# Activations of the 256-column stages moved to rows of 1024 bytes, at the down stage's distance from the weights

## What is computed

```python
# first block, L = 272 columns up to fox's queries, then 256
h = h + (rms_norm(o, g_out) * silu(z)) @ a_w_out          # o, z from rms_norm(h) @ a_w_in (HGRN2)
k, v, fl = rms_norm(h, kv_norm) @ kv_w                    # shared keys and values
u = rms_norm(h, b_norm) @ b_w_in                          # queries and gates: 256 columns
h = h + (forgetting_attention(u, k, v, fl) * silu(z)) @ b_w_out
# second block, 256 columns
proj = rms_norm(x, norm1) @ w_in + b_in
x = x + concat(conv_group(proj), window_attention(proj)) @ w_out
# PEER: 8 heads pick 16 of 128 x 128 experts; u and v have 16384 rows of 2048
xn = rms_norm(x, norm2)
q = xn @ peer_w_q
a = gelu(xn @ peer_u.T) * gate        # done for all 16384 rows, gate 0 where not picked
x = x + a @ peer_v
```

## The kernel before

| tensor | begins at | modulo 512 | row step |
|---|---|---|---|
| `whi` | 57856 | 0 | 512 per kk |
| `wlo` | 24416 | 352 | 512 per kk |
| `e_coef_hi` | 22240 | 224 | 1024 |
| `e_coef_lo` | 144128 | 256 | 1024 |
| `e_coef_first` | 228096 | 256 | one row |
| `xb_hi`, `xb_lo` | 91648, 109056 | 0, 0 | 1088 per kk |
| `xa_hi`, `xa_lo` | 126464, 143872 | 0, 0 | 1088 per kk |

## Time and profile before

### The profile page before, as it was taken

How to read it: one execution, slowest core, us unless ns; L and a number is a source line. 1 busy time by engine, 2 the same in 40 slices (tenths; PEclk the granted TensorE clock), 3 DMA queues, 4 the chain that set the end, 5 groups by cost and what they waited for, 6 DMA issues and landing times.

```text
span 3040.3 us, 63437 instructions
## 1 busy us (share of the span) xinstructions
PE 3000.6 (99%) x25230; PEld 2943.4 (97%) x25230; DVE 1947.1 (64%) x3277; ACT 1616.5 (53%) x2611; POOL 665.5 (22%) x293
## 2 busy tenths in 40 slices
PE   9999998999999999989999999999999999999999
PEld 8999998999999998869999999999999999999999
DVE  6777776644544568758777798554458865555544
ACT  6777675566788643455444444444444444444443
POOL 3333333444444432115444300000000000000000
PEclk9999999999999999989999999999999999999999
DMA  5444443544444454325555544555554455555554
GB/s 207 151 152 149 141 152 132 176 166 166 167 139 150 146 180 153 113 78 196 173 187 182 180 148 159 182 192 186 187 193 155 153 189 184 190 183 193 181 192 166
DMA packets 72432, 506.67 MB, mean 167 GB/s; under 512 B 7920, under 2 KB 10480, under 8 KB 11504
## 3 DMA queue, kind: packets, MB, share of 16 engines
q1 hardware_dynamic: 71728, 503.16, 48.4%
q10 hardware_dynamic: 576, 1.72, 0.2%
HBM read 502.75 MB, written 2.10 MB: 166 GB/s over the span
## 4 chain that ended last, share of the span: by engine, by line
PE 95%; DVE 3%; ACT 2%; issue 0%; DMA 0%; SPq 0%; DVEq 0%; ACTq 0%
PE bank L451 12%; PE bank L450 12%; PE bank L452 12%; PE bank L464 6%; PE bank L2312 4%; PE banks L2312 4%; PE bank L2313 4%; PE banks L2313 4%; PE bank L2314 4%; PE banks L2314 4%; PE bank L2085 3%; PE bank L2086 3%; PE bank L2087 3%; PE banks L2085 3%; PE banks L2086 3%; PE banks L2087 3%
## 5 line engine op out<-in xcount | busy, mean ns | idle before, releaser
L427 ACT ACTIVATE whi<-raw 128x1024 fp32r<-128x1024 f32 x896 | 941.8, 1058 | 988.5 <-PE bank L452 366.1
L434 DVE TENSOR_TENSOR wlo<-raw,whi 128x1024 fp32r<-128x1024 f32 x667 | 851.4, 1287 | 429.2 <-ACT whi L427 428.2
L434 POOL TENSOR_TENSOR wlo<-raw,whi 128x1024 fp32r<-128x1024 f32 x231 | 608.4, 2634 | 937.0 <-ACT whi L427 925.8
L450 PE MATMUL bank<-xa_hi,whi 128*128 128x272 f32 (+1 forms) x1984 | 576.0, 290 | 4.2 <-DVE wlo L434 4.1
L451 PE MATMUL bank<-xa_lo,whi 128*128 128x272 f32 (+1 forms) x1984 | 567.5, 286 | 0.0
L452 PE MATMUL bank<-xa_hi,wlo 128*128 128x272 f32 (+1 forms) x1984 | 566.5, 286 | 0.0
L450 PEld LDWEIGHTS bank<-xa_hi,whi 128*128 128x128 f32 x1984 | 372.8, 188 | 6.7 <-issue 5.1
L451 PEld LDWEIGHTS bank<-xa_lo,whi 128*128 128x128 f32 x1984 | 374.1, 189 | 1.3
L452 PEld LDWEIGHTS bank<-xa_hi,wlo 128*128 128x128 f32 x1984 | 372.9, 188 | 0.0
L450 PE MATMUL bank<-xb_hi,whi 128*128 128x256 f32 (+1 forms) x1120 | 317.9, 284 | 1.5 <-DVE wlo L434 1.5
L451 PE MATMUL bank<-xb_lo,whi 128*128 128x256 f32 (+1 forms) x1120 | 316.4, 283 | 0.0
(11 more groups left out here) (458 smaller groups left out, 6787.9 us busy)
## 6 DMA issues: line engine op xcount, KB each, us to landing
raw<-in_w SPq DMA_DIRECT2D x250, 1024.0 KB, 4.8
raw<-in_v SPq DMA_DIRECT2D x128, 1024.0 KB, 5.3
raw<-in_u SPq DMA_DIRECT2D x96, 1024.0 KB, 4.9
hT<-in_hT SPq DMA_DIRECT2D x4, 544.0 KB, 6.9
out<-hT SPq DMA_DIRECT2D x8, 256.0 KB, 2.4
raw<-in_w SPq DMA_DIRECT2D x2, 512.0 KB, 6.1
r_keys<-in_keys ACTq DMA_DIRECT2D x1, 1024.0 KB, 4.9
c_mask<-in_masks ACTq DMA_DIRECT2D x1, 320.0 KB, 3.0
```

The lines of the kernel that those rows point to most:

```text
L427: act.activation(whi[:, (2 * t.q + half) % 4, :], raw[:, t.q, half * 1024:(half + 1) * 1024], ACT.Copy).then_inc(w_hi_done, 1)
L434: eng.tensor_tensor(wlo[:, t.q, at], raw[:, t.q, at], whi[:, slot, :].bitcast(F32), ALU.subtract).then_inc(w_lo_done[half], 1)
L450: te.matmul(ps, hi, x[0][:, kk, cols], start=(kk == 0), stop=False)
```

## The change

Four tensors are added, `yb_hi`, `yb_lo`, `ya_hi`, `ya_lo`, each 16 rows of 256 columns (1024 bytes). They lie over the memory of `xb_hi`, `xb_lo`, `xa_hi`, `xa_lo`, 56 or 64 elements (224 or 256 bytes) behind their start: `yb_hi` begins at 91872 (224 modulo 512), `yb_lo` at 109312 (256), `ya_hi` at 126688 (224), `ya_lo` at 144128 (256). Nothing else moves. Every stage of 256 columns with split data now writes and reads these; the stages of 272 columns keep `xa` and `xb`. No instruction, wait or transfer is added, dropped or put elsewhere. In the keys and values stage the split of the next stage's data is made for 256 columns instead of 272; the convolution's copies of two rows become contiguous.

```diff
+SQUARE_GAP = {"hi": 56, "lo": 64}
...
-        xb = (tensor(ctx, "xb_hi", [P, KT, L], F32R), tensor(ctx, "xb_lo", [P, KT, L], F32R))
+        def rows_of(name, part):
+            with ExitStack() as st:
+                tensor(st, f"{name}_{part}_gap", [P, SQUARE_GAP[part]])
+                return tensor(st, f"{name}_{part}", [P, KT, SEQ], F32R)
+
+        yb_hi = rows_of("yb", "hi")
+        xb_hi = tensor(ctx, "xb_hi", [P, KT, L], F32R)
+        yb = (yb_hi, rows_of("yb", "lo"))
+        xb = (xb_hi, tensor(ctx, "xb_lo", [P, KT, L], F32R))
         innermost = ExitStack()
-        xa = (tensor(innermost, "xa_hi", [P, KT, L], F32R), tensor(innermost, "xa_lo", [P, KT, L], F32R))
+        ya_hi = rows_of("ya", "hi")
+        xa_hi = tensor(innermost, "xa_hi", [P, KT, L], F32R)
+        ya = (ya_hi, rows_of("ya", "lo"))
+        xa = (xa_hi, tensor(innermost, "xa_lo", [P, KT, L], F32R))
...
-        OUT = ((T_AOUT, xb, cols_all, "kv_norm", xa, 1), (T_BOUT, xa, cols_q, "norm1", xn1, 3),
-               (T_WOUT, xa, cols_q, "norm2", xb, 4))
+        OUT = ((T_AOUT, xb, cols_all, "kv_norm", xa, 1), (T_BOUT, ya, cols_q, "norm1", xn1, 3),
+               (T_WOUT, ya, cols_q, "norm2", yb, 4))
...
-                        act.activation(at3(xb[0], h), at3(hT, h), ACT.Copy, scale=par("b_norm", h))\
+                        act.activation(at3(yb[0], h), at3(hT, h, cols_q), ACT.Copy, scale=par("b_norm", h))\
...
-                        ve.scalar_tensor_tensor(at3(xb[1], h), at3(hT, h), par("b_norm", h),
-                                                at3(xb[0], h).bitcast(F32), ALU.mult, ALU.subtract)\
+                        ve.scalar_tensor_tensor(at3(yb[1], h), at3(hT, h, cols_q), par("b_norm", h),
+                                                at3(yb[0], h).bitcast(F32), ALU.mult, ALU.subtract)\
...
-                        project(te, Tile(T_QZ, i, 2 * u), xb, cols_q)
+                        project(te, Tile(T_QZ, i, 2 * u), yb, slice(0, SEQ))
...
-                        act.activation(xa[0][:, k:k + 2, 0:SEQ], c.cv[:, k:k + 2, :], ACT.Copy)\
+                        act.activation(ya[0][:, k:k + 2, :], c.cv[:, k:k + 2, :], ACT.Copy)\
...
-                        project(te, t, xb, slice(0, SEQ), skipped=2, ps=route_ps(t.q))
+                        project(te, t, yb, slice(0, SEQ), skipped=2, ps=route_ps(t.q))
...
-                    te.matmul(ps, hi, xb[0][:, kk, 0:SEQ], start=(kk == 0), stop=False)
-                    te.matmul(ps, hi, xb[1][:, kk, 0:SEQ], start=False, stop=False)
-                    last = te.matmul(ps, lo, xb[0][:, kk, 0:SEQ], start=False, stop=(kk == KT - 1))
+                    te.matmul(ps, hi, yb[0][:, kk, :], start=(kk == 0), stop=False)
+                    te.matmul(ps, hi, yb[1][:, kk, :], start=False, stop=False)
+                    last = te.matmul(ps, lo, yb[0][:, kk, :], start=False, stop=(kk == KT - 1))
```

More of the change, by code:

```diff
@@ L489, in out_piece @@
         def out_piece(te, base, tile, kks):
-            x, n = (xb, L) if base == T_AOUT else (xa, SEQ)
+            x, n = (xb, L) if base == T_AOUT else (ya, SEQ)
             t = Tile(base, 0, tile)
@@ L1128, in body @@
                     if within(h, HEADS):
-                        project(te, Tile(T_QZ, i, 2 * u + 1), xb, cols_q)
+                        project(te, Tile(T_QZ, i, 2 * u + 1), yb, slice(0, SEQ))
                         te.wait_ge(qsq_done, h + 1)
@@ L1194, in body @@
                         lone(act)
-                        act.activation(at3(xa[0], h - 2, slice(0, SEQ)), one3(f.mm[:]), ACT.Copy)\
+                        act.activation(at3(ya[0], h - 2), one3(f.mm[:]), ACT.Copy)\
                             .then_inc(x_hi_done, 1)
@@ L1253, in body @@
                         ve.wait_ge(x_hi_done, SPLITS[T_QZ] + h - 1)
-                        ve.tensor_tensor(at3(xa[1], h - 2, slice(0, SEQ)), one3(f.mm[:]),
-                                         at3(xa[0], h - 2, slice(0, SEQ)).bitcast(F32), ALU.subtract)\
+                        ve.tensor_tensor(at3(ya[1], h - 2), one3(f.mm[:]),
+                                         at3(ya[0], h - 2).bitcast(F32), ALU.subtract)\
                             .then_inc(x_split, 1)
@@ L1466, in wout_piece @@
                 hi, lo = whi[:, slot, k * P:(k + 1) * P], wlo[:, t.q, kk * P:(kk + 1) * P]
-                te.matmul(ps, hi, xa[0][:, kk, 0:SEQ], start=(kk == 8), stop=False)
-                te.matmul(ps, hi, xa[1][:, kk, 0:SEQ], start=False, stop=False)
-                last = te.matmul(ps, lo, xa[0][:, kk, 0:SEQ], start=False, stop=(kk == KT - 1))
+                te.matmul(ps, hi, ya[0][:, kk, :], start=(kk == 8), stop=False)
+                te.matmul(ps, hi, ya[1][:, kk, :], start=False, stop=False)
+                last = te.matmul(ps, lo, ya[0][:, kk, :], start=False, stop=(kk == KT - 1))
             if k0 == KT - 2:
@@ L1629, in swa_scalar @@
                     act.wait_ge(S.o, j + 1)
-                    act.activation(xa[0][:, CONV_T + j, 0:SEQ], PS_O, ACT.Copy).then_inc(x_hi_done, 1)
+                    act.activation(ya[0][:, CONV_T + j, :], PS_O, ACT.Copy).then_inc(x_hi_done, 1)
                 j = s - 1
@@ L1656, in lo_att @@
                 ve.wait_ge(x_hi_done, x_count("att", j))
-                ve.tensor_tensor(xa[1][:, CONV_T + j, 0:SEQ], PS_O, xa[0][:, CONV_T + j, 0:SEQ].bitcast(F32),
+                ve.tensor_tensor(ya[1][:, CONV_T + j, :], PS_O, ya[0][:, CONV_T + j, :].bitcast(F32),
                                  ALU.subtract).then_inc(x_split, 1)
@@ L1661, in lo_conv @@
                 ve.wait_ge(x_hi_done, x_count("conv", k))
-                ve.tensor_tensor(xa[1][:, k:k + 2, 0:SEQ], c.cv[:, k:k + 2, :],
-                                 xa[0][:, k:k + 2, 0:SEQ].bitcast(F32), ALU.subtract).then_inc(x_split, 2)
+                ve.tensor_tensor(ya[1][:, k:k + 2, :], c.cv[:, k:k + 2, :],
+                                 ya[0][:, k:k + 2, :].bitcast(F32), ALU.subtract).then_inc(x_split, 2)
             def conv_gated(k):
@@ L1822, in body @@
                     if static(i) and i + s == 0:
-                        project(te, t, xb, slice(0, SEQ), skipped=2, ps=route_ps(t.q), halves=(0,))
+                        project(te, t, yb, slice(0, SEQ), skipped=2, ps=route_ps(t.q), halves=(0,))
                         out_sum(te, T_WOUT, SEQ)
-                        project(te, t, xb, slice(0, SEQ), skipped=2, ps=route_ps(t.q), halves=(1,))
+                        project(te, t, yb, slice(0, SEQ), skipped=2, ps=route_ps(t.q), halves=(1,))
                     else:
-                        project(te, t, xb, slice(0, SEQ), skipped=2, ps=route_ps(t.q))
+                        project(te, t, yb, slice(0, SEQ), skipped=2, ps=route_ps(t.q))
                     if p - 1 in KEY_AT:
```

## The result

The changed kernel takes 3052.84 us in the median (3049.04 to 3054.74, 7 runs) against 3040.36 us before (3039.73 to 3043.2, 7 runs): ratio 1.0035, 95% interval 1.0025 to 1.0044. It is **slower by 0.35%**; 3032.9 was forecast, with a range up to 3038.0. The profiled execution took 3052.84 us, its span 3051.0.

What follows compares the result with a forecast made beforehand. TensorE, busy 99% of the span, was taken as the bound. 9792 matmuls at 0.97 ns gave 9.5 us less, all other parts nothing: 3032.9 us forecast from a median of 3042.43, range 3029.4 to 3038.0.

Steps and rivals of the forecast that it cites:

- TensorE's spacing sets the time: Whole kernel: TensorE busy 3000.6 us, 99% of the span, so time comes or goes only through its matmul spacing.
- The distance between data and weights is worth some ns a matmul, modulo 512: Split-weight products: address distance modulo 512 changes matmul time; up against down stage spacing differs by 0.97 ns a matmul.
- Equal distance, equal spacing; 9792 x 0.97 ns: 3264 triples of 256 columns on `xa` and `xb` get the down stage's distances and pace: 9.5 us less.
- Untouched: the down stages: Down stages, like the 272-column and fp32 products, were to stay as before.
- Keys and values, convolution copies: Narrower splits in keys and values worth nothing on the path, 0.3 us if uncovered; contiguous convolution copies taken as zero.
- Nothing happens: Rival: data and weights are read without touching each other, address cannot matter, time stays at 3042.4; chance 6%.
- Given back at other engines: Rival: query and gate, routing, first up keep their length behind other engines; 5.2 us returned, 3038.1; chance 10%.
- The third rival: 256-column stages: the constant distance is a bad one, 7 ns a triple more, 23 us, or 3065; chance 4%.

Runs made afterwards that it cites:

- the map: Changed kernel, each of the 64 down tiles reading data from another start within `yb`, coefficients left out; 346.6 to 361.8 ns a triple, no total time given.
- the second map: The edit with another data start per down tile, hi data another 256 bytes on; 126 of 128 tiles repeat within 0.3 ns, no total time given.
- The smooth entry: Changed kernel with `e_coef_first` at 224 modulo 512 instead of 256; 3043.57 us, ratio 1.0004, ten runs in two heaps.
- the split matmul: Kernel before, first product in every fourth down tile issued as two of 128 columns; 3057.13 us, ratio 1.0051.
- half of the change: Kernel before with only `ya` changed, for both output projections; stages on `xb` as before; 3041.22 us, ratio 1.0000.

## Why the prediction was wrong

- *TensorE's spacing sets the time.* Right: 3011.9 of 3051.0 us, no new wait. For `e_col` in the first up stage TensorE waits 1.9 us in two times, the longest 1.7, against 1.8 and 1.6 before; the 1.8 in the earlier trace rows is the sum of the two and not the longest.
- *The distance between data and weights is worth some ns a matmul, modulo 512.* Right in that the address matters, and now measured: 346.6 to 361.8 ns a triple over the map. The 512 was a wrong reading. After four rows the data have moved on by 4 x 1088 = 4352 bytes, which is 256 modulo 512 and no multiple of 512; the pattern that repeats there already spoke for 256, and the second map showed it for the hi data. Whether the distance to the weights counts or the start of the data alone is not shown: the weights lay still in every run.
- *Equal distance, equal spacing; 9792 x 0.97 ns.* **This step failed.** It rests on "In the down stage the distance is the same for every row, and so is the time". The time was the same for every row because the whole stage ran in one rhythm. 348.9 ns is one of two spacings that this pair of addresses has; the two profiled down stages had both entered it, and that is no property of the addresses alone. Where the fast rhythm ruled, the term was right: the end of the second up stage has the forecast 1206 matmuls and the forecast durations, 348.9 ns a triple against 351.7. But some two fifths of the settled triples on `ya` and `yb` ran at 355.5, 3.8 ns above the old rows, which took most of the gain back. From the first triple's start to the last one's, queries and gates take as long as before, the two output projections 0.8 us more each, routing 0.4 more, the up stages 0.6 and 2.4 less, where 1.5, 0.65 each, 2.2, 1.5 and 3.0 us were to be saved: together 1.0 us less instead of 9.5.
- *Untouched: the down stages.* **Wrong in the same step.** Nothing in them moved, yet what runs ahead of them did: 6.7 + 6.7 us, more than the whole loss of 10.7 us in the span. The smooth entry brings the first one back to 1206, and the split matmul makes the kernel before slow without any move.
- *Keys and values, convolution copies.* Right: in the same 207 us TensorE is busy for 206.14 with 1619 matmuls, as before, and ScalarE's copies of two rows take 632 ns in the median in both kernels.
- *The rivals.* "Nothing happens" falls with the map. The Trainium skill's page "SBUF — State Buffer", section "Who interferes with whom", gives TensorE two independent read ports, for data and for weights, and says that TensorE never waits on anyone. The trace does not agree with what the prediction drew from that, a pace that no address changes: a triple takes 346.6 to 361.8 ns over addresses. No run shows whether the read ports are where this time arises. "Given back at other engines" falls too: no stage has a new wait. The third rival, with 4%, had the sign, but neither the mechanism nor the place: no bad distance, but a bad rhythm of a distance that can be good, and most of the loss in the down stages, which this rival too held untouched. Its 7 ns a triple were counted from the old rows; the slow rhythm lies 3.8 ns above them. No rival had a pace that depends on what ran before. The proper question to the profile would have been whether anything between the triples (line 2074, the products of the attention) would hit the new stages in the middle.
- *Open.* What in the entry picks the rhythm. The same kind of disturbance turns fast into slow and slow into fast in routing and in the up stages; in the queries and gates of the changed kernel two kinds take turns, and one leads to fast each time, the other to slow; a cut matmul leads to slow each time. All six profiled entries into a down stage from the old rows (the kernel before, the cut matmul, half of the change) led to 348.9; why is not explained either. That every run of the kernel before does the same is not shown, but its times in all the comparisons lie within 4.3 us, less than one slow down stage costs.

## What to carry to other kernels

A spacing read from one stage, however constant, is the spacing of one execution of one sequence; before it is carried to other stages, see whether a harmless disturbance (one matmul cut in two) leaves it where it is. Where data rows and weight rows keep a fixed distance, look for a distance with a single rhythm. One run with one tile per distance gives the map, but a few equal readings there do not prove a single rhythm; that takes a run with the real disturbances. Rows whose distance changes from row to row did not split into two rhythms here: within some twelve triples after every disturbance the old rows came back to their one pattern, 351.7 ns in the mean, between 348.9 and 355.5.

## What the runs showed that was not expected

- TensorE's pace at a fixed pair of addresses has several stable values: 348.9 and 355.5 ns a triple at 224 and 256; 346.7, 353.3 and 360.0 at 448 and 352; only 350.0 at 288 and 320, in the one profile of it. Stage after stage keeps one for as long as 64 tiles, over 360 us.
- At 448 and 352 the three lie 6.7 ns apart: over three triples, 1040, 1060 and 1080 ns.
- The pace depends on the start of the hi data modulo 256 bytes, not 512: 126 of 128 tiles agree after a shift by 256.
